# mLSTM layer of a hybrid decoder step: prompt states copied by another engine, sample rows finished by pairs of heads, the output projection's first row blocks placed beside the last rows

## What is computed

```
xm, z = split(xn @ w_in)              # 2 x 2048 columns
xc    = silu(causal_conv4(xm))
q, k, v = block_diagonal(xc), block_diagonal(xc), block_diagonal(xm)
per head and chunk:
  num = w_intra @ v + w_inter * (q @ C)      # C: 512x512 state
  den = sum(w_intra) + w_inter * (q @ n)
  h   = num / max(|den|, exp(-m_t))
  C_new = decay * C + (k * w_state)^T v      # an output: 8 sample states and 1 prompt state per head
  n_new = decay * n + sum(k * w_state)
h = h * rsqrt(mean(h*h) + eps) * norm_w      # per head of 512
y = (h + skip * xc) * silu(z)
x = x + rmsnorm(y @ w_out)                   # w_out: 2048 x 1024
```

## Time and profile before

| | |
|---|---|
| median of 3 runs | 1199.1 us (1193.4 to 1199.39) |
| the profiled execution's own time | 1193.88 us |
| its span | 1191.9 us, mean granted clock 0.967 |
| PE busy | 1096.5 us, 92% of the span |
| VectorE (DVE) busy | 668.2 us, 56% |
| ScalarE (ACT) busy | 534.3 us, 45% |
| GpSimd (POOL) busy | 149.9 us, 13% |
| mLSTM loop and sample rows | from about 697 to 910 us of the span |

### The profile page before, as it was taken

How to read it: one execution, slowest core, us unless ns; L and a number is a source line. 1 busy time by engine, 2 the same in 40 slices (tenths; PEclk the granted TensorE clock), 3 DMA queues, 4 the chain that set the end, 5 groups by cost and what they waited for, 6 DMA issues and landing times.

```text
span 1191.9 us, 21680 instructions
## 1 busy us (share of the span) xinstructions
PE 1096.5 (92%) x8493; PEld 959.0 (80%) x8493; DVE 668.2 (56%) x953; ACT 534.3 (45%) x874; POOL 149.9 (13%) x204
## 2 busy tenths in 40 slices
PE   4998998767999999999899999999986999999996
PEld 4986877557999999999899865554635999999995
DVE  4568675422456544345996557685766366444333
ACT  5322635223455554334565344453523366553431
POOL 5133000000002220001300411000000003220000
PEclk9998999888999999999999999998996999999998
DMA  9697897798525555553643139899996534554541
GB/s 336 221 336 256 312 346 283 280 351 332 160 91 176 162 169 162 161 171 126 248 160 125 53 117 398 317 386 309 363 352 226 172 106 164 169 162 159 163 137 40
DMA packets 92262, 260.94 MB, mean 219 GB/s; under 512 B 8836, under 2 KB 9860, under 8 KB 91800
## 3 DMA queue, kind: packets, MB, share of 16 engines
q1 hardware_dynamic: 91320, 257.92, 61.7%
q0 software_dynamic: 432, 1.29, 0.4%
q10 hardware_dynamic: 432, 0.65, 0.2%
HBM read 218.10 MB, written 41.73 MB: 218 GB/s over the span
## 4 chain that ended last, share of the span: by engine, by line
PE 81%; DVE 10%; DMA 3%; ACT 3%; issue 2%; SPq 0%; POOL 0%; POOLq 0%; DVEq 0%; ACTq 0%
PE ps L1887 19%; PE ps L1888 19%; PE ps L1889 19%; PE ps L2367 3%; PE ps L2342 3%; PE ps L2370 2%; PE ps L1999 2%; DVE w_lo L1140 2%; DMA kv_a<-in_kv 2%; PE ps L2080 2%; PE ps L2240 2%; DVE rstd L1167 1%; PE ps L2284 1%; PE ps L2247 1%; PE ps L1981 1%
## 5 line engine op out<-in xcount | busy, mean ns | idle before, releaser
L1140 DVE TENSOR_TENSOR w_lo<-w_raw,w_hi 128x1024 fp32r<-128x1024 f32 x232 | 285.3, 1237 | 215.3 <-ACT w_hi L680 214.3
L680 ACT ACTIVATE w_hi<-w_raw 128x1024 fp32r<-128x1024 f32 x232 | 241.8, 1053 | 206.8 <-PE ps L1889 193.9
L1887 PE MATMUL ps<-xin_hi,w_hi 128*128 128x288 f32 x1016 | 308.4, 304 | 25.1 <-DVE w_lo L1140 23.2
L1888 PE MATMUL ps<-xin_lo,w_hi 128*128 128x288 f32 x1016 | 304.9, 300 | 0.0
L1889 PE MATMUL ps<-xin_hi,w_lo 128*128 128x288 f32 x1016 | 304.3, 299 | 0.0
L1887 PEld LDWEIGHTS ps<-xin_hi,w_hi 128*128 128x128 f32 x1016 | 195.0, 192 | 37.4 <-DVE w_lo L1140 20.0
L1888 PEld LDWEIGHTS ps<-xin_lo,w_hi 128*128 128x128 f32 x1016 | 194.0, 191 | 0.8 <-issue 0.2
L1889 PEld LDWEIGHTS ps<-xin_hi,w_lo 128*128 128x128 f32 x1016 | 193.8, 191 | 0.0
L1888 PE MATMUL ps<-hid_lo,w_hi 128*128 128x288 f32 x512 | 152.6, 298 | 0.0
L1889 PE MATMUL ps<-hid_hi,w_lo 128*128 128x288 f32 x512 | 151.9, 297 | 0.0
L1887 PE MATMUL ps<-hid_hi,w_hi 128*128 128x288 f32 x512 | 151.4, 296 | 0.0
(11 more groups left out here) (394 smaller groups left out, 1699.7 us busy)
## 6 DMA issues: line engine op xcount, KB each, us to landing
w_raw<-in_weights SPq DMA_DIRECT2D x232, 512.0 KB, 3.7
cring<-in_C SPq DMA_DIRECT2D x64, 512.0 KB, 6.3
out_Cs<-cring SPq DMA_DIRECT2D x64, 512.0 KB, 6.0
kv_a<-in_kv SPq DMA_DIRECT2D x60, 448.0 KB, 5.5
kv_b<-in_kv SPq DMA_DIRECT2D x60, 448.0 KB, 5.8
out_Cp<-cring SPq DMA_DIRECT2D x8, 512.0 KB, 5.5
kv_w<-in_kv SPq DMA_DIRECT2D x8, 448.0 KB, 5.3
x<-in_x SPq DMA_DIRECT2D x1, 1152.0 KB, 7.5
```

What stands on the lines that cost most here:

```text
L680: act.activation(w_hi[:, l % UM], w_raw[:, l % W_SLOTS], ACT.Copy).then_inc(hi_ready, 1)
L1140: dve.tensor_tensor(w_lo[:, l % W_SLOTS], w_raw[:, l % W_SLOTS], w_hi[:, l % UM], ALU.subtract).then_inc(lo_ready, 1)
L1887: pe.matmul(out, w_hi[:, j, ws], hi, start=start and kk == 0, stop=False)
L1888: pe.matmul(out, w_hi[:, j, ws], lo, start=False, stop=False)
```

## The change

It moves and rewrites work inside the mLSTM loop and behind it. No output changes its meaning.

- `new_state` on VectorE no longer copies prompt halves; ScalarE does it (`prompt_state`) in blocks 2 and 3, with a semaphore `p_new` of its own; `made(i)` says which semaphore and value stand for item i.
- PE makes the row squares in block 2, ahead of the outer products, instead of in block 3. ScalarE's SiLU moves to block 0 and its root to block 2; VectorE's reciprocal and norm product move to block 2, skip and gate to block 3.
- Sample rows are finished for heads 0 and 1 inside head 2, and for heads 2 and 3 after the loop. The unscaled `hs` is transposed (into bank 3), the product with norm_w and z is folded beforehand, and the row scale comes in by a product: a diagonal of scales times a matrix of ones gives a broadcast in PSUM, with which the rows are multiplied.
- In the last head: casts of weights 0 and 1 in blocks 2 and 3, `y1_hi` and `y1_lo` of its prompt rows in block 4, and `sum_groups` ahead of the last half product.
- The first four steps of OUT_C start when heads 0 and 1 are complete; the last transposes and the scale product stand ahead of step 0 and step 1. The 16 steps are written out instead of looped.

The core of the diff:

```diff
+        def made(i):
+            h, r = divmod(i, ITEMS)
+            b, half = ORDER[r]
+            if b == NB:
+                return p_new, 2 * h + half + 1
+            return c_new, 2 * NB * h + sum(1 for j in range(r + 1) if ORDER[j][0] < NB)
...
-                sp.wait_ge(c_new, i + 1)
+                sp.wait_ge(*made(i))
...
-            sp.wait_ge(y1_ready, NH + 1)
+            sp.wait_ge(y1_ready, NH)
...
+            def sample_roots(c):
+                two = stok[:, 3, 2 * c:2 * c + 2]
+                act.wait_ge(hs_mean, c + 1)
+                act.activation(two, two, ACT.Sqrt, bias=tiny[0:NS, 0:1], scale=1.0 / DH).then_inc(hs_std, 1)
+            def prompt_state(h, half):
+                i = item(h, NB, half)
+                s = i % C_SLOTS
+                act.wait_ge(c_mm, i + 1)
+                if i >= C_SLOTS:
+                    act.wait_ge(c_out[s], 16 * (i // C_SLOTS))
+                act.activation(cring[s], ps[:, banks_of(i):banks_of(i) + HD2, :], ACT.Copy).then_inc(p_new, 1)
+            def sample_high(c):
+                ms = slice(2 * ET * c, 2 * ET * c + 2 * ET)
+                act.wait_ge(y1s_full, c + 1)
+                act.activation(y1_hi[:, ms, SEQ:T], hs_f[:, ms], ACT.Copy).then_inc(y1s_hi, 1)
             def chunk(h, b):
                 if b == 0:
                     act.wait_ge(den_psum, h + 1)
                     act.activation(stok[:, 0, h:h + 1], ps[0:NS, 3, SEQ:SEQ + 1], ACT.Abs)
                     act.activation(dn, ps[:, 3, 0:SEQ], ACT.Abs).then_inc(den_abs, 1)
+                    act.activation(z[:, ET * h:ET * h + ET], z[:, ET * h:ET * h + ET], ACT.Silu).then_inc(z_ready, 1)
...
                 if b == 2:
-                    act.activation(z[:, ET * h:ET * h + ET], z[:, ET * h:ET * h + ET], ACT.Silu).then_inc(z_ready, 1)
-                if b == 3:
                     act.activation(dn, staged(h, "mean")[:, 0:SEQ], ACT.Sqrt, bias=tiny[:, 0:1], scale=1.0 / DH
                                    ).then_inc(stage_read_a, 1)
+                    if h == 2:
+                        sample_roots(0)
+                if b in (2, 3):
+                    if h + 1 == NH:
+                        act_hi(b - 2, 0, STEP0[OUT_C])
+                    prompt_state(h, b - 2)
                 if b == 4 and h + 1 < NH:
                     qk(h + 1)
                 if b == 5 and h + 1 < NH:
                     keys_by_token(h + 1)
                     own_keys(h + 1)
-                if b == 6:
-                    if h + 1 < NH:
-                        values_by_token(h + 1)
+                if b == 6 and h + 1 < NH:
+                    values_by_token(h + 1)
+                    if h == 2:
+                        sample_high(0)
+                if b == (6 if h + 1 < NH else 4):
                     act.wait_ge(y1_full, h + 1)
                     act.activation(y1_hi[:, ET * h:ET * h + ET, 0:SEQ], hT, ACT.Copy).then_inc(y1_hi_ready, 1)
...
+            sample_roots(1)
+            sample_high(1)
...
-                if b < NB:
-                    dve.wait_ge(c_in[s], 16 * loads(i))
-                    last = dve.scalar_tensor_tensor(cring[s], cring[s],
-                                                    bc[:, h % 2, R_DECAY + b:R_DECAY + b + 1], new, ALU.mult, ALU.add)
-                else:
-                    if i >= C_SLOTS:
-                        dve.wait_ge(c_out[s], 16 * (i // C_SLOTS))
-                    last = dve.tensor_copy(cring[s], new)
-                last.then_inc(c_new, 1)
+                dve.wait_ge(c_in[s], 16 * loads(i))
+                dve.scalar_tensor_tensor(cring[s], cring[s], bc[:, h % 2, R_DECAY + b:R_DECAY + b + 1], new,
+                                         ALU.mult, ALU.add).then_inc(c_new, 1)
+            def sample_stats(c):
+                two = slice(2 * c, 2 * c + 2)
+                order.after(dve.tensor_tensor(stok[:, 2, two], stok[:, 0, two], tokg_s[:, 1, two], ALU.max))
+                order.after(dve.reciprocal(stok[:, 2, two], stok[:, 2, two]))
+                dve.wait_ge(hs_sq, 2 * c + 2)
+                order.after(dve.tensor_tensor(stok[:, 3, two], stok[:, 1, two], stok[:, 2, two], ALU.mult))
+                dve.tensor_tensor(stok[:, 3, two], stok[:, 3, two], stok[:, 2, two], ALU.mult).then_inc(hs_mean, 1)
+            def sample_scales(c):
+                two = slice(2 * c, 2 * c + 2)
+                dve.wait_ge(hs_std, c + 1)
+                order.after(dve.reciprocal(stok[:, 3, two], stok[:, 3, two]))
+                order.after(dve.tensor_tensor(stok[:, 4, two], stok[:, 3, two], stok[:, 2, two], ALU.mult))
+                if c:
+                    dve.wait_ge(hs_bc, c)
+                dve.tensor_tensor(hs_diag, ident[0:NS, 0:NS].unsqueeze(1).to_broadcast([NS, 2, NS]),
+                                  stok[:, 4, two].unsqueeze(2).to_broadcast([NS, 2, NS]), ALU.mult).then_inc(hs_scaled, 1)
+            def of_heads(c):
+                return slice(2 * ET * c, 2 * ET * c + 2 * ET)
+            def by_row(name, c):
+                first = AT[name] + 2 * ET * c
+                return par[:, first:first + 2 * ET].unsqueeze(2).to_broadcast([P, 2 * ET, NS])
+            def sample_folds(c):
+                xs, zs = xcc[:, of_heads(c), SEQ:T], z[:, of_heads(c), SEQ:T]
+                dve.wait_ge(z_ready, 2 * c + 2)
+                order.after(dve.tensor_tensor(xs, xs, by_row("skip", c), ALU.mult))
+                order.after(dve.tensor_tensor(xs, xs, zs, ALU.mult))
+                order.after(dve.tensor_tensor(zs, zs, by_row("norm_w", c), ALU.mult))
+            def sample_gates(c):
+                dve.wait_ge(hst_ready, c + 1)
+                order.after(dve.tensor_tensor(hs_f[:, of_heads(c)], ps[:, 3, 0:256].rearrange("p (m t) -> p m t", t=NS),
+                                              z[:, of_heads(c), SEQ:T], ALU.mult))
+            def sample_rows(c):
+                xs, rows_f = xcc[:, of_heads(c), SEQ:T], hs_f[:, of_heads(c)]
+                heads_f = rows_f.rearrange("p (h e) t -> p h e t", h=2)
+                scale = ps[:, 3, 256:256 + 2 * NS].rearrange("p (h t) -> p h t", h=2).unsqueeze(2)
+                dve.wait_ge(hs_bc, c + 1)
+                order.after(dve.tensor_tensor(heads_f, heads_f, scale.to_broadcast([P, 2, ET, NS]), ALU.mult))
+                dve.tensor_tensor(rows_f, rows_f, xs, ALU.add).then_inc(y1s_full, 1)
+            def sample_low(c):
+                dve.wait_ge(y1s_hi, c + 1)
+                dve.tensor_tensor(y1_lo[:, of_heads(c), SEQ:T], hs_f[:, of_heads(c)], y1_hi[:, of_heads(c), SEQ:T],
+                                  ALU.subtract).then_inc(y1s_ready, 1)
...
+                    if h == 2:
+                        sample_stats(0)
                 if b == 1:
                     new_n(h)
                 if b == 2:
-                    new_state(h, NB, 0)
-                if b == 3:
-                    new_state(h, NB, 1)
-                if b == 4:
                     dve.wait_ge(stage_read_a, reads(use(h, "mean"))[1])
                     order.after(dve.reciprocal(dn, dn))
                     for e in range(ET):
                         order.mark(dve.scalar_tensor_tensor(hT[:, e], hT[:, e], pcol("norm_w", ET * h + e), dn,
                                                             ALU.mult, ALU.mult))
-                if b == 5:
+                    if h + 1 == NH:
+                        dve_lo(0, 0, STEP0[OUT_C])
+                if b == 3:
                     order.wait()
                     for e in range(ET):
                         m = ET * h + e
                         order.mark(dve.scalar_tensor_tensor(hT[:, e], xcc[:, m, 0:SEQ], pcol("skip", m), hT[:, e],
                                                             ALU.mult, ALU.add))
-                    if h + 1 < NH:
-                        keys_low(h + 1)
                     order.wait()
                     dve.wait_ge(z_ready, h + 1)
                     dve.tensor_tensor(hT, hT, z[:, ET * h:ET * h + ET, 0:SEQ], ALU.mult).then_inc(y1_full, 1)
+                    if h >= 2:
+                        sample_folds(h - 2)
+                    if h == 2:
+                        sample_gates(0)
+                        sample_scales(0)
+                    if h + 1 == NH:
+                        dve_lo(1, 0, STEP0[OUT_C])
+                if b == 5 and h == 2:
+                    sample_rows(0)
+                if b == 5 and h + 1 < NH:
+                    keys_low(h + 1)
                 if b == 6 and h + 1 < NH:
                     values_low(h + 1)
-                if b == 7:
+                if b == 7 and h == 2:
+                    sample_low(0)
+                if b == (7 if h + 1 < NH else 4):
                     dve.wait_ge(y1_hi_ready, h + 1)
                     dve.tensor_tensor(y1_lo[:, ET * h:ET * h + ET, 0:SEQ], hT, y1_hi[:, ET * h:ET * h + ET, 0:SEQ],
                                       ALU.subtract).then_inc(y1_ready, 1)
```

(73 more changed lines are left out.)

36 lines of the change are left out of this document (6 added, 30 removed).

## The result

| kernel | median us | lowest to highest | runs |
|---|---|---|---|
| before | 1193.53 | 1189.14 to 1199.39 | 8 |
| after | 1183.01 | 1179.88 to 1187.85 | 8 |

The ratio is 0.9904, 95% interval 0.9881 to 0.9927: some 11 us faster. The profiled execution of the changed kernel took 1187.85 (span 1185.9) and is the slowest of its eight. Against the one of before, 1193.88, that is 6.0 less, but its first head begins 5.1 later, at 697.64 against 692.54, behind code that the change does not touch. So what follows counts inside the heads: from one head's scores to the next, from head 3's scores to the last update L, and from L to the root of the norm behind the projection.

A forecast was written before the change was run, and what follows sets the result against it. PE was taken to bound ordinary heads, VectorE the last head, followed by an 11.0 us serial stretch. Terms 1.5 - 1.2 + 2.1 + 11.0 + 0 = 13.4 us off 1193.88 gave 1180.5, range 1173 to 1190.

The forecast's parts named there:

- the clock: Granted PE clock in the last head and output projection: between +2.6 and -3.3 us, taken as 0.
- The two levels: Three runs of the kernel before, read as two levels some 6 us apart; on the upper, the changed median about 1186.
- Copies to ScalarE: Prompt-state copies in each head: 1.00 us instead of 1.22, PE's holes shrink 0.49 a head, 1.5 us in three heads.
- Row squares one block earlier: Row squares ahead of the prompt products: PE's sum unchanged; only in head 3 is an update late, by 0.27 us.
- Head 2 pays: Finishing the first sample rows inside head 2 (transposes, scale matmul, wait, cast) costs 1.2 us, bounds 0 to 2.5.
- The last head: From the second prompt product's end to the last update: 15.0 us instead of 17.2, a gain taken as 2.1.
- Behind the last update: Output projection runs as if begun at the last update, not 11.0 us later: gain 11.0 us, bounds 8 to 11.6.
- rival (c): Clock holds throughout and the projection opens at full clock: gain 16.0, 1177.9 us, or 1173 without falls; chance 0.25.
- rival (a): Clock falls in each head plus a half-clock tail eat the gain: gain 0 to 6, 1188 to 1194 us; chance 0.10.
- One sign of being right: Heads other than the last were to stay within 1 us of before, with head 2 the longest.
- (b): Weights 2 and 3 or a ScalarE cast come late; projection step 2 waits 4 to 6 us: 1184 to 1187; chance 0.12.
- (d): Slower: half clock through blocks 1 to 4 of every head doubles the prompt products: 1200 us and above; chance 0.04.

The follow-up runs named there:

- spread: Changed kernel with the second half of the key sums (8 one-column products) and new n moved from block 1 to block 2: 1175.93 us, on another chip 1176.73.
- before_spread: Kernel before, with only the second half of the key sums and the new n moved from block 1 to block 2: 1189.86 us, ratio 0.9961.
- late_start: Changed kernel, but the first four steps of the output projection wait for all rows, as before the change: 1191.25 us, ratio 0.9957.

## Why the prediction was right, point by point

1180.5 was forecast and 1183.0 measured, inside the range, faster as expected. By medians the gain is 10.5 us, where the forecast had 13.4. The sum of the work was right to 0.7 us (12.7 for 13.4, the terms below); the term that was mis-sized is **the clock**, put at 0: it came out at about -3. The base was a lucky choice: of the times shown I took the profiled execution's own, 1193.88, and not the median of three, 1199.1. The median of all eight is 1193.53; from 1199.1 the same gain would have given 1185.7. The two levels that I saw in three runs are not there either: 29 runs of the kernel before lie between 1187.0 and 1203.2 with no empty place in the middle.

- **Copies to ScalarE.** 1.00 us forecast, 1.024 measured; 0.49 a head forecast, 0.38 measured (50.99 to 50.61). But to price it by its holes alone was too narrow: beside the early norm chain it is worth 10 us, falls included, by the run with the copies behind the chain.
- **Row squares one block earlier.** No cost of its own in heads at full clock (50.59, 50.61). In head 3 PE waits 0.33 for the update; forecast 0.27.
- **Head 2 pays.** Without a fall 52.17, and before 50.94: 1.23 net of the holes, so 1.6, where 1.2 was forecast. The wait for the scales is 0.48 (in the run spread), not 0.2.
- **The last head.** Product's end to L: 15.0 forecast, 14.2 measured. Head 3 up to L, without falls at the end of block 1, shrinks by 2.4 (47.06 to 44.70, before_spread to spread), where 2.1 was forecast. Some of that is clock: before_spread's last 9.3 us ahead of L are at 0.50, as before's last 7.1 are. The runs do not separate it.
- **Behind the last update.** Start at L - 0.69 (forecast L - 0.75), the scale product 0.45 (0.15), step 2 waiting 0.4 (0.6), so 11.0 + 0.7 - 0.45 - 0.4, some 10.8 for 11.0: small misses that nearly cancel. L to root fell by 13.2; the other 2.4 fits the projection that opens at 0.13 a matmul instead of 0.24.
- **The clock.** Two errors of opposite sign. In the tail it stayed up: rival (c) in part, +2.4 of its 2.6. In the heads rival (a) came in part. Against the runs late_start (head 2) and spread (the others), heads 0 to 3 lost 1.6, 3.2, 3.2 and 2.8, together 10.9; before lost 3.1 in head 2 and 1.6 in head 3 against before_spread, and under 1 in head 0 by the fall at 693.7, about 5.5. So -5.4 + 2.4 = -3.0. The work is 3 x 0.38 for the copies, less 1.6 for head 2, 2.4 for the last head and 10.8 behind L: 12.7. And 12.7 - 3.0 = 9.7 is what the two profiles differ by from the first scores to the root (272.66 and 263.00); that it closes proves little, since the 2.4 behind L is a remainder. In which heads the clock falls hangs on the execution. One sign of being right failed with it: heads 1 and 2 were to stay within 1 us of before and took 2.8 and 1.3 more.
- **Falls and gaps.** The Trainium skill (TensorE: Matmul & The Clock Gate, "HAM oscillation") ties such falls to gaps between matmuls. This fits the tail of both profiles of the changed kernel, where no hole is over 1.3 us and the clock stayed up; at 764.5 it does not hold, with PE busy 2.00 of 2.00 before and in the fall. And holes as short as these did not keep the clock safe: with the same 1.2 us hole it fell in the last head of late_start and of sums_block2.
- **The sum without falls at the end of block 1.** before_spread and spread differ by this change alone, and neither has such a fall. From 1189.86 to 1176.73 on one chip is 13.1 us, for 13.4 forecast; from the first scores to the root their profiles take 266.98 and 253.96, 13.0 less. That this meets the 13.4 so closely is in part chance, since other clock is left in it on both sides: the fall in spread's head 2 costs 1.8 (53.97 for 52.17), and before_spread has the one in head 0 and the 23.9 us at half clock.
- **Rivals (b) and (d).** Weight 2 landed 1.0 us ahead of its cast (910.7 and 911.8), where 1.2 to spare was forecast; half clock through blocks 1 to 4 of every head did not come.

What is shown: taking eight one-column products out of block 1 takes the falls there away (none in 12 heads of three profiles; 25 in 40 with them in), and both kernels become faster by more than the noise. Pair by pair it is 7 heads in 8 against none in 8 for the changed kernel and 2 in 4 against none in 4 for the one before. With all sixteen out, one fall in four heads came a little later, at the row squares. What is only argued: that the row squares in block 2 make the falls likelier (22 of 28 heads with them there, 3 of 12 without, over kernels that differ in other things too). In each of the 22 the fall begins ahead of the row squares of its own head, so how they bring it on is open. So is why one execution of the same order had none, and what it is about the small products there that matters to the clock.

## What to carry to other kernels

When a change moves small products beside other small products, price their stretch at full and at half clock, and look for a place to spread them: 8 products moved by one block gave some 6.6 us here (1182.9 to 1176.3), with nothing removed. A copy given to another engine may be worth too little to be told alone (0.9994) and 10 us together with the order that it allows; test it in both orders. Before an engine is relieved, see what stands right behind it: here slower skip products, a load and the clock took its place. And take several profiles before a fall of the clock is priced: one execution says little about the next.

## What had not been expected of the hardware

- TensorE fell to 0.50 for 3.4 or 6.8 us with no gap in its work, in some executions of an order of work and not in others; a fall of 6.8 us costs 3.2, one of 3.4 half of that (53.04 for 51.40 in head 0).
- GpSimd's 128x1024 subtraction (2.35 us) held up VectorE's skip products, which read two tensors in SBUF (3.42 for 1.67), and not its updates, which read one there and one in PSUM: an earlier one (877.59 to 879.95) began inside two updates, which took 2.47 as they do without it. The reciprocal behind them, which has one input, in SBUF, overlapped its last 0.9 us and took 1.75, the same as elsewhere. It is one case of each.
